# Two mixers' small parts moved: query rotation by transfers, and the bias table's product in another block

## The reference

```python
def mla_mixer(h, w_in, q_norm, kv_norm, w_uq, w_ukv, w_o):
    proj = h @ w_in                      # 384 + 256 + 32 columns
    c_q, c_kv, k_rope = ...
    q = (rmsnorm(c_q, q_norm) @ w_uq).reshape(B, S, 16, 64 + 32)
    kv = (rmsnorm(c_kv, kv_norm) @ w_ukv).reshape(B, S, 16, 64 + 64)
    q_rope = apply_rotary(q[..., 64:], cos, sin)      # x1*cos - x2*sin, x1*sin + x2*cos
    k_rope = apply_rotary(k_rope, cos, sin)           # one for all 16 heads
    s = (q_nope . k_nope + q_rope . k_rope) * scale   # causal softmax, then . v, then @ w_o
```

## Time and profile before

| What | us |
|---|---|
| Median of 3 runs | 1409.35 |
| The profiled execution | 1408.82 |
| Its span, first to last instruction | 1407.0 |
| PE busy in the span | 1394.5 (99%) |
| DVE busy | 915.5 (65%) |
| ACT busy | 740.8 (53%) |
| POOL busy | 73.3 (5%) |

### The profile page before, as it was taken

One profiled execution on the slowest core, in us unless ns is written; L12 is line 12 of the kernel. 1 busy time (PEld: TensorE's weight loads), 2 busy tenths in 40 slices (PEclk: granted clock), 3 DMA queues, 4 the chain that ended last, 5 costly groups with the idle time before them and its releaser, 6 DMA issues.

```text
span 1407.0 us, 22782 instructions
## 1 busy us (share of the span) xinstructions
PE 1394.5 (99%) x8944; PEld 1263.5 (90%) x8944; DVE 915.5 (65%) x1169; ACT 740.8 (53%) x912; POOL 73.3 (5%) x113
## 2 busy tenths in 40 slices
PE   9999999999999999999999999999999999999998
PEld 8989999999988888899888888888889999888886
DVE  5555787675666665677666666666567676665656
ACT  7556663344355444557554444544545558554454
POOL 2000010010010000010120000100000002200000
PEclk9999999999999999999999999999999999999999
DMA  8544441255545555462375555655555410555552
GB/s 324 194 144 147 157 144 61 91 195 186 193 141 201 197 189 186 173 201 85 124 271 196 194 200 175 236 193 195 192 179 183 151 56 2 200 204 181 198 187 89
DMA packets 34771, 239.67 MB, mean 170 GB/s; under 512 B 3914, under 2 KB 4058, under 8 KB 6928
## 3 DMA queue, kind: packets, MB, share of 16 engines
q1 hardware_dynamic: 32832, 231.39, 46.9%
q0 software_dynamic: 1440, 6.67, 1.4%
q10 hardware_dynamic: 432, 0.66, 0.2%
HBM read 237.10 MB, written 1.08 MB: 169 GB/s over the span
## 4 chain that ended last, share of the span: by engine, by line
PE 96%; DVE 1%; ACT 1%; issue 0%; DMA 0%; POOL 0%; POOLq 0%; ACTq 0%; DVEq 0%
PE ps L736 22%; PE ps L706 16%; PE ps L708 16%; PE ps L707 16%; PE ps L744 11%; PE ps L1037 3%; PE ps L1011 2%; PE ps L1021 1%; PE ps L1355 1%; PE ps L2944 1%; PE ps L2952 1%; PE ps L645 1%; PE ps L2956 1%; PE ps L3120 1%; PE ps L827 1%
## 5 line engine op out<-in xcount | busy, mean ns | idle before, releaser
L413 DVE TENSOR_TENSOR low<-raw,high 128x2048 fp32r<-128x2048 f32 (+2 forms) x194 | 440.1, 2270 | 202.2 <-ACT high L407 199.7
L407 ACT ACTIVATE high<-raw 128x2048 fp32r<-128x2048 f32 (+1 forms) x197 | 372.0, 1890 | 41.0 <-PE ps L708 36.5
L736 PE MATMUL ps<-nt,high 128*128 128x512 f32 x1344 | 320.1, 390 | 0.0
L736 PEld LDWEIGHTS ps<-nt,high 128*128 128x128 f32 x1344 | 249.0, 188 | 50.6 <-issue 0.9
L706 PE MATMUL ps<-nt,high 128*128 128x256 f32 x656 | 186.3, 284 | 0.0
L708 PE MATMUL ps<-nt,low 128*128 128x256 f32 x656 | 185.1, 282 | 0.0
L707 PE MATMUL ps<-nt,high 128*128 128x256 f32 x656 | 185.0, 282 | 0.0
L744 PEld LDWEIGHTS ps<-nt,low 128*128 128x128 f32 x1344 | 167.5, 189 | 3.6
L744 PE MATMUL ps<-nt,low 128*128 128x256 f32 x1344 | 168.6, 283 | 0.0
L706 PE MATMUL ps<-high,hth 128*128 128x512 f32 x320 | 124.5, 389 | 0.0
L707 PE MATMUL ps<-low,hth 128*128 128x512 f32 x320 | 124.5, 389 | 0.0
(11 more groups left out here) (425 smaller groups left out, 2151.7 us busy)
## 6 DMA issues: line engine op xcount, KB each, us to landing
raw<-in_stream SPq DMA_DIRECT2D x215, 1024.0 KB, 4.9
late<-in_w POOLq DMA_DIRECT2D x1, 2048.0 KB, 9.4
scr<-bias_by_distance POOLq DMA_DIRECT2D x1, 2048.0 KB, 12.8
scr<-in_mem SPq DMA_DIRECT2D x2, 512.0 KB, 5.1
raw<-in_stream SPq DMA_DIRECT2D x4, 256.0 KB, 5.9
raw<-in_stream SPq DMA_DIRECT2D x2, 512.0 KB, 7.0
x<-in_x SPq DMA_DIRECT2D x1, 1024.0 KB, 8.2
con<-in_con SPq DMA_DIRECT2D x1, 592.0 KB, 9.0
```

Source lines behind the costliest of these rows:

```text
L407: nc.scalar.activation(high_of(t, slice(0, n)), raw[t % SLOTS][:, 0:n], ACT.Copy).then_inc(w_high, 1)
L413: nc.vector.tensor_tensor(low_of(t, slice(0, n)), raw[t % SLOTS][:, 0:n], high_of(t, slice(0, n)).bitcast(F32), ALU.subtract).then_inc(w_l ...
L736: last = nc.tensor.matmul(r3(bank, 2), w[:, k, P * j:P * j + P], nt[:, :, k, :], start=first and k == 0, stop=not first and k == KC - 1, s ...
```

## The change

Three things are done.

- Queries. The rotary columns of all 16 heads are gathered in one tile, uq0 (512 columns, 4 blocks of 4 heads), the plain ones in two, uq1 and uq2; a fourth tile is gone. DVE multiplies each bank of uq0 by a cosine table and by a sine table, over all 128 rows (`ml_turned`). Eight transfers from ACT's queue, of 32 partitions x 4 heads x 256 tokens (128 KB) each, put the cosine products on rows 64 to 96 and the sine products on rows 96 to 128 of each head. No addition is made. Instead the rotary key is laid down twice, on rows 64 to 96 in its order and on rows 96 to 128 with its halves exchanged, and the scores contract over 128 rows and not 96; the transfer that copies it to the heads is twice as large. The plain rows of uq1 and uq2 hold two heads in a block; ACT copies the one on rows 0 to 64, DVE the other.
- Bias table. Its product, ACT's copy and the first transfer move from the third feed-forward block to the first one's start; the product takes the place of three idle products, which become two of half the width (one more, of the full width, becomes two of half).
- Small ones. Two semaphores for two loads at 90 us become one; a table in SBUF goes, two come.

The diff, cut to its core:

```diff
-    t += ["mlain0", "mlain1", "mlain2"] + [f"uq{j}" for j in range(4)] + ["uk", "uv"]
+    t += ["mlain0", "mlain1", "mlain2"] + [f"uq{j}" for j in range(3)] + ["uk", "uv"]
...
+        ml_turned = [r3(ml["y"][:, 1024 * n:1024 * n + 1024], 4) for n in range(2)]
...
-            UNITS.append(dict(products=[(r3(ml["q"], MLA_H)[0:96, h, :], r3(ml["k"], MLA_H)[0:96, h, :])],
+            UNITS.append(dict(products=[(r3(ml["q"], MLA_H)[:, h, :], r3(ml["k"], MLA_H)[:, h, :])],
...
             first_gate()
+            if f == 0:
+                pe.wait_ge(ns_linec, 1)
             up(tb + 1, n0)
             pe_late_root(pe, name)
-            if f == 2:
-                pe.wait_ge(ns_tbl, 32)
-                tbl = nt_["tbl"][0:BIAS_ROWS, 0:NSA_H]
-                nc.tensor.matmul(ps[1][0:NSA_H, :], tbl, nt_["hot"][0:BIAS_ROWS, :], start=True, stop=True)\
-                    .then_inc(ns_line, 1)
...
@@ gpsimd
+            pool.wait_ge(w_used, TILE[f"up{BRANCH[-1]}1"] + 1)
+            pool.dma_start(nt_["hot"][0:BIAS_ROWS, :], A["hot"]).then_inc(ns_tbl, 16)
+            pool.dma_start(nt_["tbl"][0:BIAS_ROWS, :], A["bucket_bias"]).then_inc(ns_tbl, 16)
...
             pool_late_root(pool, ch, "f0")
+            pool.wait_ge(ns_linec, 1)
+            pool.dma_start(line, nt_["line"][0:NSA_H, :]).then_inc(ns_lined, 16)
...
-            pool.dma_start(mk_[64:96, :, :], rep(mlc["kr"][64:96, S:2 * S], MLA_H)).then_inc(ml_krd, 16)
+            pool.dma_start(mk_[64:128, :, :], rep(mlc["kr"][64:128, S:2 * S], MLA_H)).then_inc(ml_krd, 16)
...
@@ scalar
-            act_norm(act, "f0")
+            act_norm(act, "f0", (0,))
+            act.wait_ge(ns_line, 1)
+            nc.scalar.activation(nt_["line"][0:NSA_H, :], ps[6][0:NSA_H, :], ACT.Copy, scale=NSA_D ** 0.5)\
+                .then_inc(ns_linec, 1)
+            act_norm(act, "f0", (1,))
...
+            act_step(act, "uq0")
+            act.wait_ge(ml_qd, 2)
             for j in range(4):
+                for n in range(2):
+                    act.dma_start(mq[64 + 32 * n:96 + 32 * n, j::4, :], ml_turned[n][32 * j:32 * j + 32])\
+                        .then_inc(ml_qrd, 16)
+            for j in (1, 2):
                 act_step(act, f"uq{j}")
...
                 for b in range(2):
                     uq_here(act, j, b)
-                    h = 4 * j + 2 * b
-                    nc.scalar.activation(mq[0:64, h:h + 2, :], r3(ps[2 * (j % 2) + b][0:64, :], 2), ACT.Copy)\
+                    h = 8 * (j - 1) + 4 * b
+                    nc.scalar.activation(mq[0:64, h:h + 4:2, :], r3(ps[2 * (j % 2) + b][0:64, :], 2), ACT.Copy)\
...
@@ vector
                 for b in range(2):
                     uq_here(dve, j, b)
-                    if j + b:
-                        dve.wait_ge(ml_qd, 2 * j + b)
-                    h = 4 * j + 2 * b
-                    rotate(ps[2 * (j % 2) + b], 2, mq[64:96, h:h + 2, :]).then_inc(ml_qd, 1)
+                    bank = ps[2 * (j % 2) + b]
+                    if j:
+                        h = 8 * (j - 1) + 4 * b
+                        nc.vector.tensor_copy(mq[0:64, h + 1:h + 4:2, :], r3(bank[64:128, :], 2)).then_inc(ml_qd, 1)
+                    else:
+                        for n, table in enumerate((cos_, sin_)):
+                            last = nc.vector.tensor_tensor(ml_turned[n][:, 2 * b:2 * b + 2, :], r3(bank, 2), rep(table, 2),
+                                                           ALU.mult)
+                        last.then_inc(ml_qd, 1)
...
@@ tensor
-            pe_idle_products(ident, causal, 3)
+            pe.wait_ge(ns_tbl, 32)
+            nc.tensor.matmul(ps[6][0:NSA_H, :], nt_["tbl"][0:BIAS_ROWS, 0:NSA_H], nt_["hot"][0:BIAS_ROWS, :], start=True,
+                             stop=True).then_inc(ns_line, 1)
+            pe_idle_products(ident, causal[:, 0:P], 2, ps[3][:, P:2 * P])
             pe_late_turn(pe, "f0", 1, range(4), 2)
-            pe_idle_products(ident, causal, 1)
+            pe_idle_products(ident, causal[:, 0:P], 2, ps[3][:, P:2 * P])
...
-            for j in range(4):
+            for j in range(3):
...
             pe.wait_ge(ml_krd, 16)
+            pe.wait_ge(ml_qrd, 16 * 8)
```

More of the change, by code:

```diff
@@ L85 @@
 GATE_AND_UP = {f"f{f}{part}{i}" for f in range(4) for part in "gu" for i in range(FT)}
-USED = {"ba": KC * P, "ng": KC * P, "uq0": 1536, "uq1": 1536, "uq2": 1536, "uq3": 1536}
+USED = {"ba": KC * P, "ng": KC * P, "uq0": 1536, "uq1": 1536, "uq2": 1536}
 TILE = {n: i for i, n in enumerate(PLAN)}
@@ L111 @@
 _at = 0
-for _n, _w in (("ident", 128), ("gains", 128), ("upto", 128), ("before", 128), ("ones", 128), ("causal", 256),
-               ("window", 256), ("rope", 256), ("rowok", 32)):
+for _n, _w in (("ident", 128), ("gains", 128), ("upto", 128), ("ones", 128), ("causal", 256),
+               ("window", 256), ("cos", 256), ("sin", 256), ("rowok", 32)):
     CON[_n] = _at
@@ L129, in constants @@
     put("upto", (j <= i) * 1.0)
-    put("before", (j < i) * 1.0)
     put("ones", np.ones((P, P)))
@@ L224, in lay_out @@
     q = wuq.reshape(MLA_QL, MLA_H, MLA_N + MLA_R)
-    q = np.concatenate([q, q[:, :, 80:96], q[:, :, 64:80]], axis=2).reshape(MLA_QL, MLA_H * P)
-    for j in range(4):
-        put(f"uq{j}", cols(q, 512 * j, 512))
+    nope, rope = (np.ascontiguousarray(v).reshape(MLA_QL, -1) for v in (q[:, :, :MLA_N], q[:, :, MLA_N:]))
+    put("uq0", cols(rope, 0, 512))
+    for j in range(2):
+        put(f"uq{j + 1}", cols(nope, 512 * j, 512))
     kv = wukv.reshape(MLA_KVL, MLA_H, 2, 64)
@@ L286, in build @@
         vec = con[:, CON["gains"]:CON["gains"] + NVEC]
-        small = sb("small", [P, 1024])
+        small = sb("small", [P, 960])
         SCR = 14336
@@ L327, in c_ @@
             return con[:, CON[name]:CON[name] + w]
-        ident, upto, before, ones = (c_(n, P) for n in ("ident", "upto", "before", "ones"))
+        ident, upto, ones = (c_(n, P) for n in ("ident", "upto", "ones"))
         causal, window = c_("causal", 256), c_("window", 256)
@@ L368, in build @@
         ns.update(carve(nl["w1"], [("kw", 2048), ("vs", 528), ("vw", 528), ("new", 512)]))
-        nt_ = carve(ns["ks"], [("hot", 512), ("tbl", 16), ("line", 512)])
+        nt_ = carve(late, [("hot", 512), ("tbl", 16)], 2304)
+        nt_["line"] = nt_["hot"]
         sems = {}
@@ L1215, in build @@
         sw_vt = xm["q"][:, 0:S]
-        gm_loaded, gm_sum, gm_vn, gm_wmask, gm_mixed, gm_y, gm_high, gm_low = (
-            s_("gm_" + n) for n in ("loaded", "sum", "vn", "wmask", "mixed", "y",
+        tables_loaded = s_("tables_loaded")
+        gm_sum, gm_vn, gm_wmask, gm_mixed, gm_y, gm_high, gm_low = (
+            s_("gm_" + n) for n in ("sum", "vn", "wmask", "mixed", "y",
                                     "high", "low"))
@@ L1250, in build @@
                                     "lm", "p", "pc", "y", "t", "u", "uc", "wc", "o0", "sc", "vnd",
-                                    "osum", "out", "level", "tap0", "bas"))
+                                    "osum", "out", "tap0", "bas"))
         kn_ = lambda t: [tok[:, t, 4 + h, :] for h in range(DN_H)]
@@ L1471, in act_ffn @@
             act_late_root(act, f"f{f}")
-            if f == 2:
-                act.wait_ge(ns_line, 1)
-                nc.scalar.activation(nt_["line"][0:NSA_H, :], ps[1][0:NSA_H, :], ACT.Copy, scale=NSA_D ** 0.5)\
-                    .then_inc(ns_linec, 1)
             up_cross(tb + 1, n0)
@@ L1733, in build @@
         (ml_chigh, ml_sum, ml_ms, ml_rs, ml_diag, ml_spread, ml_rows, ml_kvm, ml_kvhigh, ml_kvlow, ml_kr,
[L1734 removed]
+         ml_krd, ml_qrd, ml_q, ml_qa, ml_qd, ml_ka, ml_kd, ml_va, ml_vd, ml_v) = (
             s_("ml_" + n) for n in ("chigh", "sum", "ms", "rs", "diag", "spread", "rows", "kvm", "kvhigh",
[L1736 removed]
+                                    "kvlow", "kr", "krd", "qrd", "q", "qa", "qd", "ka", "kd", "va", "vd", "v"))
         def uq_here(eng, j, b):
@@ L1818, in _ @@
                     sp.dma_start(row[:], A["row"]).then_inc(row_here, 16)
-            with sp.Fori(2, (NT - 1) // SLOTS) as i:
+            with sp.Fori(2, NT // SLOTS) as i:
                 for c in range(SLOTS):
@@ L1902, in _ @@
             pool_late_root(pool, ch, "f2")
-            pool.wait_ge(ns_linec, 1)
-            pool.dma_start(line, nt_["line"][0:NSA_H, :]).then_inc(ns_lined, 16)
             pool.wait_ge(ns_lined, 16)
@@ L3040, in _ @@
                 for b in range(2):
-                    if j >= 2:
-                        pe.wait_ge(ml_qa, 2 * (j - 2) + b + 1)
-                        pe.wait_ge(ml_qd, 2 * (j - 2) + b + 1)
+                    if j == 2:
+                        pe.wait_ge(ml_qd, b + 1)
                     for c in range(2):
@@ L3074, in _ @@
             weights_here(pe, t)
-            pe.wait_ge(ml_qa, 8)
-            pe.wait_ge(ml_qd, 8)
+            pe.wait_ge(ml_qa, 4)
+            pe.wait_ge(ml_qd, 6)
             def v_part(n, bank):
```

62 lines of the change are left out of this document (27 added, 35 removed).

## The result

| | us |
|---|---|
| After, median of 8 runs | 1413.86 (1413.02 to 1415.74) |
| Before, 8 runs | 1409.46 (1408.74 to 1411.32) |
| Ratio | 1.0033, 95% interval 1.0023 to 1.0043 |
| The profiled execution after | 1414.62, span 1412.8 |

The change makes the kernel slower, by 4.4 us or 0.3%; the interval leaves out 1.

What follows compares the result with a forecast made beforehand. PE was taken to bound the kernel, busy 1394.5 of 1407.0 us. Bias product -0.96, later uk +1.7, clock's fall +1.8 gave +2.5 on 1408.82, so 1411.3, with 0.53 to the median 1411.9 us; range 1406.4 to 1414.0.

Steps and rivals of the forecast that it cites:

- the price of the eight issues: Query transfers on ACT ahead of its uk split: 0.45 us each, 3.6 in all, bounds 2.9 and 5.4.
- The rival on the other side: ACT's issues cost 0.68 us each, 5.4 in all; uk at 636.4, clock falls, 1413.7 us; chance 0.15.
- PE's two gains: One query tile fewer, 4.2 us, and the bias table's product out of the third feed-forward block, 0.96 us.
- The end of the table products: DVE's last cosine and sine product in the first mixer, which ACT awaits before issuing, ends at 621.15 us.
- The chain through ACT and DVE: From ACT's split of uk at 624.75 through DVE's splits and scaled features to ml_kvlow at 634.4 us.
- uk at 634.6: First mixer: PE's uk products start at 634.6 us, 1.7 us later than before.
- The idle time: PE stands idle between the end of uq2 and the start of uk for 5.7 us.
- The clock's fall: PE's clock drops to half rate in the idle before uk, 4.6 us after work stops; price 1.8 us.
- The rival of a stall without a fall: PE idles before uk but its clock stays at full rate; 1410.1 us; chance 0.25.
- The rival of issues that do not hold ACT: Only ml_qd's wait delays ACT: uk at 631.0 after 2.1 us idle, clock stays, 1406.5 us; chance 0.12.
- The keys' transfer: Rotary keys to the heads, twice the bytes: at most 11.8 us, landing at 643.1, before PE wants them at 643.3.
- the two rules: Trainium skill pages: idle gaps risk half clock rate; an issue's time is usually small beside its transfer, about 50 ns dispatch.

Runs made afterwards that it cites:

- experiment 9: The changed kernel with query transfers issued by SyncE, keys' rows ahead of uv's split, and two stream tiles held until the keys' transfer landed; 1403.17 us.
- experiment 4: The changed kernel with the rows of the keys' features ahead of uv's split on ACT and DVE, issues still on ACT; 1411.76 us.
- experiment 12: The changed kernel with query transfers on SyncE and two stream tiles held until the keys' transfer landed, uv's split still ahead of the keys' rows; 1405.4 us.
- experiment 2: The changed kernel with 16 idle products on PE between uq2 and the wait for ml_kvlow; 1411.75 us.
- experiment 6: The changed kernel with query transfers issued by GpSimd, no wait for ml_qd on ACT, and the keys' rows ahead of uv's split; 1411.3 us.
- experiment 5: The changed kernel with the eight query transfers issued by GpSimd, ACT's wait for ml_qd kept; 1408.65 us.
- experiment 8: The changed kernel with query transfers issued by SyncE between stream tiles, no wait or issue on ACT, keys' rows ahead of uv's split; 1407.31 us.
- experiment 3: The changed kernel with its eight query transfers cut into sixteen of half the size, the same bytes in all; 1418.52 us.
- experiment 7: The changed kernel with GpSimd issuing the keys' transfer first, the eight query transfers behind it, and keys' rows ahead of uv's split; 1413.6 us.

## Why the prediction was wrong

**The step that failed is the price of the eight issues.** The prediction took 0.45 us each, 3.6 in all, with bounds of 2.9 and 5.4. From the first issue's start to ACT's split were 6.7 us, 0.84 each, above the upper bound. Seven of the eight were 0.66 apart, near SP's 0.68, and one took 1.87. The row on ACT itself, from which the 0.45 came, was a single issue in front of a table load, and says little about a row of them; the row of four in succession on SP was the nearer one. That an issue in a row costs more than one alone shows on SyncE too: 0.60 and 0.34 us for the same tile (experiment 9). The rival on the other side (0.68 each), given 0.15, should have been the forecast: I had costed the issue by its engine and should have costed it by its pattern. That its 1413.7 meets the measured 1413.9 is in part luck. It had uk at 636.4; uk came at 638.4, 2.0 later, of which 1.3 are the issues (6.7 us and not 5.4) and 0.5 the start. The profiled executions differ by 5.8 us, where that rival had 4.3, and the medians only by 4.4.

The further steps:

- PE's two gains: right. A tile of 4.2 us is gone, and the table's product gave back 1.1 us in the profile, 0.96 expected. Nothing moved at 407 us: the products in front of the new ones start at 406.57 (before 406.08), those behind the first block's start at 417.34 (before 416.87), 0.5 us later both times.
- The end of the table products was forecast at 621.15 and was 621.64, by the 0.5 us of the start of the kernel (scatter, as said above).
- The chain through ACT and DVE: right in its order and in each length. From ACT's split at 628.37 to ml_kvlow at 638.11 are 9.7 us; the prediction had 624.75 to 634.4, 9.65. Experiments 4 and 12 confirm uv's split in it.
- uk at 634.6: was 638.37. Of the 3.8 us, 3.1 are the issues, 0.5 the start.
- The idle time: 8.8 in place of 5.7.
- The clock's fall: right that it comes, and its price of 1.8 us was 1.5 by the changed kernel's timeline and 1.8 by experiment 2. But it did not take the 4.6 us of the kernel's end; it came 2.5 us after the last product. The rival of a stall without a fall is out: each fall seen came sooner than 5.7 us after the last product, and in experiment 6 the clock fell with only 4.0 us of idle time. With 2.5 us (experiment 5) it did not.
- The rival of issues that do not hold ACT: out. Experiment 5 shows what the time is without them.
- The keys' transfer: bounded at 11.8 us, 9.4 measured, and so hidden, because uk came late. Moved forward, in experiments 5, 6 and 8, it took 12 to 14 us, and what I said of it (twice the row) covered neither the stream nor the queries ahead of it.

Of the two rules, that of DMA: Bandwidth & Descriptors in the Trainium skill, "Issuing engines are not separate DMA queues", has two halves. That DMAs of all engines share the same 16 DMA engines agrees with experiments 8 and 9: on a queue of its own the keys' transfer still took 12.0 us with the stream and 9.1 without. That the issue's time is usually small beside the transfer is no guide here: 0.65 us of the issuing engine for a transfer that lands in 2.5, and 6.6 for eight.

## What to carry to other kernels

A DMA issue takes time of the engine that issues it, in a row on ACT here about 0.65 us, for 128 KB and for 64 KB alike, and a row of them is priced from a row of them. Put such a row on a queue whose engine has nothing behind it that the bounding engine waits for. And once a stage is shortened, look at the transfers that its slowness had hidden: prefetch that is not needed for 30 us can be held back for the 9 us in which a transfer on the path needs all the DMA engines. Look first at what was issued just ahead of that transfer, on whatever queue.

## What was not expected of the hardware

- One issue of a row takes 1.2 to 1.9 us in place of 0.65: the fifth in each row of eight on ACT and in the row of sixteen, there once only, and the seventh in each row of eight on SyncE (1.2 to 1.7). Its cause was not tried.
- GpSimd issues the same eight in 4.4 us (0.55 each), SyncE in 5.9 to 6.4, ACT in 5.9 to 6.6.
- The clock's fall came 2.5 us after the last product in the changed kernel, 2.9 or 3.0 in experiments 3, 4 and 6, 4.4 in experiment 7 and 4.6 at the kernel's end. It came back after 3.1 (experiment 3) to 4.0 us of work (the changed kernel), but after 5.7 in experiment 6. No single delay fits the rows.
- It also fell with no such gap: at about 107.2 us in the profiled execution of experiment 5, where the longest wait of PE from 90 to 108 us was 0.6 us, and it stayed at half for some 7 us. What set it off is open.
- A transfer that writes 1 MB to 64 partitions in pieces of 1 KB keeps all DMA engines busy at 154 GB/s, where the stream's tiles of 1 MB landed in 4.9 us. In experiment 8, where it stood behind a tile, it moved 0.89 MB in 4 us (632 to 636), a faster pace; why is open.
- Bytes issued first moved first, across queues (experiment 8: 0.66 MB of SyncE's queue and none of GpSimd's from 629 to 631, the keys' transfer having been issued at 626.9). It is not a rule for every mix: in experiment 7 both queues moved bytes from 638 to 643, 0.97 MB on SyncE's and 0.40 MB on GpSimd's.
